# Mixing stages of a two-block network: order of ScalarE's root and table load, VectorE's rests and scans, and the size of the sum's pieces

## The reference, cut to what matters

```python
def hybrid_mixer(h, ...):
    proj = h @ w_in                       # 1024 -> 512 + 1280 + 1280 + 1024 + 1024
    u_pool, u_lru, u_gelu, g_logits = ...
    y_pool = pool_mixer(u_pool, ...) @ w_pool_up
    v = causal_depthwise_conv(u_lru, conv_w, conv_b)
    y_lru = (rg_lru(v, ...) * gelu(u_gelu)) @ w_lru_up
    g = sigmoid(g_logits)                 # g_pool, g_lru
    return (g_pool * y_pool + g_lru * y_lru) @ w_out

def rg_lru(u, w_a, b_a, w_x, b_x, lam):   # per head of 128, 10 heads
    r = sigmoid(u @ w_a + b_a);  i = sigmoid(u @ w_x + b_x)
    log_a = -8 * r * softplus(-lam)
    a = exp(log_a);  mult = sqrt(-expm1(2 * log_a))
    h_t = a_t * h_{t-1} + mult_t * i_t * u_t   # a scan over the tokens
    return h
```

## Time and profile before

| | us |
|---|---|
| median of 3 runs (lowest to highest) | 3142.77 (3141.48 to 3145.83) |
| profiled execution | 3143.91 |
| its span | 3142.2 |
| TensorE busy | 3015.3 (96%) |
| VectorE busy | 1566.0 (50%) |
| ScalarE busy | 1071.4 (34%) |
| GpSimd busy | 224.5 (7%) |

### The profile page before, as it was taken

The page is one execution under the profiler, slowest core; times in us unless marked ns, Lnnn a source line. Parts: engine busy times, 40 slices in busy tenths (PEclk is TensorE's granted clock), DMA queues, the critical chain, the costliest instruction groups (busy, mean ns, idle before and its releaser), DMA issues.

```text
span 3142.2 us, 42567 instructions
## 1 busy us (share of the span) xinstructions
PE 3015.3 (96%) x17368; PEld 2082.8 (66%) x17368; DVE 1566.0 (50%) x2551; ACT 1071.4 (34%) x1514; POOL 224.5 (7%) x262
## 2 busy tenths in 40 slices
PE   6999999999998989999999998999999999999998
PEld 5985444444443964444444445998879989897898
DVE  6764334444443673322234224557765555578554
ACT  3432222222223552222222224335543343464433
POOL 0300111111110001111111110000000000000000
PEclk9989999999999989999999999999999999999999
DMA  9836689999995537787879875554345555445453
GB/s 340 240 141 266 258 332 370 360 384 367 368 361 210 178 121 281 296 314 308 327 307 355 322 295 188 188 187 160 136 162 186 187 182 187 165 143 187 154 188 107
DMA packets 274332, 770.43 MB, mean 245 GB/s; under 512 B 36929, under 2 KB 186577, under 8 KB 210929
## 3 DMA queue, kind: packets, MB, share of 16 engines
q1 hardware_dynamic: 236016, 715.17, 61.6%
q0 software_dynamic: 29232, 45.43, 4.2%
q10 hardware_dynamic: 8912, 7.40, 0.8%
HBM read 924.08 MB, written 1.05 MB: 294 GB/s over the span
## 4 chain that ended last, share of the span: by engine, by line
PE 88%; DVE 7%; ACT 3%; issue 1%; DMA 1%; DVEq 0%; ACTq 0%
PE G L1421 21%; PE U L1441 6%; PE B L1441 5%; PE G L1207 5%; PE G L1208 5%; PE G L1209 5%; PE U L1207 4%; PE U L1208 4%; PE U L1209 4%; PE Y L1207 4%; PE Y L1208 4%; PE Y L1209 4%; PE Y L1452 2%; PE Y L1451 2%; PE M L1401 2%; PE U L1401 1%
## 5 line engine op out<-in xcount | busy, mean ns | idle before, releaser
L1796 DVE TENSOR_TENSOR part_lo<-ring,part_hi 128x2048 fp32r<-128x2048 f32 x240 | 547.8, 2288 | 389.8 <-ACT part_hi L868 388.1
L1421 PE MATMUL G<-wide,gathered 128*64 128x512 f32 x2368 | 680.9, 595 | 0.0
L868 ACT ACTIVATE part_hi<-ring 128x2048 fp32r<-128x2048 f32 x240 | 459.4, 1915 | 492.0 <-PE Y L1209 288.4
L1421 PEld LDWEIGHTS G<-wide,gathered 128*64 128x64 f32 x2368 | 207.4, 137 | 257.7 <-issue 257.7
L1421 PE MATMUL G<-arena,gathered 128*64 128x512 f32 x704 | 312.4, 596 | 0.0
L1207 PE MATMUL G<-h_hi,part_hi 128*128 128x256 f32 x1024 | 296.6, 290 | 10.9 <-DVE h_lo L1844 10.9
L1208 PE MATMUL G<-h_lo,part_hi 128*128 128x256 f32 x1024 | 295.1, 288 | 0.0
L1209 PE MATMUL G<-h_hi,part_lo 128*128 128x256 f32 x1024 | 294.7, 288 | 0.0
L1207 PE MATMUL U<-h_hi,part_hi 128*128 128x256 f32 x1024 | 289.8, 283 | 0.4 <-ACT arena L1158 0.3
L1208 PE MATMUL U<-h_lo,part_hi 128*128 128x256 f32 x1024 | 289.5, 283 | 0.0
L1209 PE MATMUL U<-h_hi,part_lo 128*128 128x256 f32 x1024 | 289.4, 283 | 0.0
(11 more groups left out here) (482 smaller groups left out, 5361.9 us busy)
## 6 DMA issues: line engine op xcount, KB each, us to landing
ring<-in_ffn_w_up_dram SPq DMA_DIRECT2D x88, 1024.0 KB, 5.3
arena<-in_moe_w_down_dram SPq DMA_DIRECT2D x86, 1024.0 KB, 7.3
wide<-in_moe_w_gate_dram SPq DMA_DIRECT2D x84, 1024.0 KB, 7.0
wide<-in_moe_w_up_dram SPq DMA_DIRECT2D x84, 1024.0 KB, 9.3
arena<-in_moe_w_gate_dram SPq DMA_DIRECT2D x44, 1024.0 KB
arena<-in_moe_w_up_dram SPq DMA_DIRECT2D x44, 1024.0 KB
ring<-in_ffn_w_down_dram SPq DMA_DIRECT2D x44, 1024.0 KB, 4.8
wide<-in_moe_w_down_dram SPq DMA_DIRECT2D x42, 1024.0 KB, 8.0
```

The source lines that it names most:

```text
L868: eng.activation(part_hi[:, n % SPLIT, :], ring[:, slot, :], ACT.Copy).then_inc(hi_ready, 1)
L1421: last = mm(bank["G"][rows], lhsT=gathered[p // 2 % 2][:, k, at:at + SLOTS], rhs=units[tile][:, :, k, :], start=(k == 0), stop=(k == K - 1 ...
L1796: eng.tensor_tensor(part_lo[:, n % SPLIT, :], ring[:, slot, :], part_hi[:, n % SPLIT, :].bitcast(F32), ALU.subtract).then_inc(lo_ready, 1)
```

## The change

On ScalarE: the rounding of unit 11 moves from behind unit 8 to behind the gates; a sigmoid of one column is put ahead of the gates; the root moves from behind the rounding of unit 20 (`q == 1`) to behind that of unit 19 (`q == 0`). On TensorE: the four banks G, U, B, M are waited for one by one, each ahead of its own piece, in units 12 and 20; unit 26 signals each of its pieces; the first unit behind the sum waits for the two halves of its rows apart. On VectorE: the low part of unit 11 moves behind the product with the gates, that of unit 21 ahead of the product with the gelu; the sum is made in four pieces of 512 columns; the first split is made in two halves of 256 columns.

```diff
-        b.book("half", f"lru_{l}")
+        b.book("half", f"lru_{l}", 3)
@@ ScalarE
-                def projected(f):
+                def projected(f, more=True):
...
-                    next_hi()
+                    if more:
+                        next_hi()
                 for f in range(IN_FIRST):
-                    projected(f)
+                    projected(f, f < IN_FIRST - 1)
+                eng.activation(stat[:, 61:62], eps[:, 0:1], ACT.Sigmoid)
                 for hd in range(LH):
...
+                next_hi()
                 projected(IN_FIRST)
...
                     wait_done(eng, unit + IN_UNITS + 4 + q)
                     next_hi()
-                    if q == 1:
+                    if q == 0:
                         eng.wait_ge(square_ready, l + 1)
                         eng.activation(tl, tl, ACT.Sqrt).then_inc(root_ready, 1)
@@ TensorE
-            def down_matmuls(parts, rows, first, end, to=None, halves=False):
+            def down_matmuls(parts, rows, first, end, to=None, halves=False, frees=None):
...
+                        if first and frees:
+                            wait_free(eng, "GUBM"[2 * t + half], frees)
...
-                for bk in "GUBM":
-                    wait_free(eng, bk, f"gp_{l}")
                 for q in range(4):
-                    down_matmuls(wait_unit(unit + 12 + q), h_rows(q), q == 0, q == 3, spread)
+                    down_matmuls(wait_unit(unit + 12 + q), h_rows(q), q == 0, q == 3, spread, frees=f"gp_{l}")
...
-                for bk in "GUBM":
-                    wait_free(eng, bk, f"yp_{l}")
...
-                                 halves=q == LRU_UNITS - 1)
+                                 halves="each" if q == LRU_UNITS - 1 else False)
...
+                def first_split(c):
+                    if c == 0:
+                        eng.wait_ge(first_rows, l + 1)
+                    else:
+                        eng.wait_ge(rows_ready, down + 7 + 1)
+                    return rows_hi[:, (down + 7) % 2, c, :], rows_lo[:, (down + 7) % 2, c, :]
+
                 for q in range(4):
-                    down_matmuls(wait_unit(unit + 27 + q), split_rows(down + 7 + q), q == 0, q == 3,
+                    down_matmuls(wait_unit(unit + 27 + q), split_rows(down + 7 + q) if q else first_split, q == 0, q == 3,
@@ VectorE
+            def split_first(src, n, read):
+                wait_done(eng, read)
+                hi, lo = rows_hi[:, n % 2], rows_lo[:, n % 2]
+                link(eng.tensor_copy(hi[:, 0, :], src[:, 0, :]))
+                eng.tensor_tensor(lo[:, 0, :], src[:, 0, :], hi[:, 0, :].bitcast(F32), ALU.subtract).then_inc(first_rows, 1)
+                eng.tensor_copy(hi[:, 1, :], src[:, 1, :]).then_inc(rows_round, 1)
+                eng.wait_ge(rows_round, n + 1)
+                eng.tensor_tensor(lo[:, 1, :], src[:, 1, :], hi[:, 1, :].bitcast(F32), ALU.subtract).then_inc(rows_ready, 1)
...
-                next_lo()
                 for hd in range(LH):
                     wait_drained(eng, gate_bank(hd), f"gates_{l}", hd // 2)
                 link(eng.tensor_tensor(ia, ia, vconv, ALU.mult))
-                next_lo(2)
+                next_lo(3)
...
+                next_lo()
                 link(eng.tensor_tensor(gl, gl, vconv, ALU.mult))
-                next_lo(2)
+                next_lo()
...
-                eng.wait_ge(half_done, b.at["half", f"lru_{l}"] + 1)
-                for t in range(TT):
-                    if t:
+                for j, (t, half) in enumerate(HALVES):
+                    if j < 3:
+                        eng.wait_ge(half_done, b.at["half", f"lru_{l}"] + j + 1)
+                    else:
                         wait_done(eng, unit + 26)
-                    for j in (2 * t, 2 * t + 1):
-                        s = mark(eng.tensor_tensor(quarter(glru, j), quarter(glru, j), quarter(Y, j), ALU.mult))
-                    eng.wait_ge(dve_step, s)
-                    eng.tensor_tensor(gpool[:, t, :], gpool[:, t, :], glru[:, t, :], ALU.add).then_inc(sum_ready, 1)
+                    hs = slice(half * HALF, (half + 1) * HALF)
+                    link(eng.tensor_tensor(quarter(glru, j), quarter(glru, j), quarter(Y, j), ALU.mult))
+                    o = eng.tensor_tensor(gpool[:, t, hs], gpool[:, t, hs], glru[:, t, hs], ALU.add)
+                    if half:
+                        o.then_inc(sum_ready, 1)
+                    else:
+                        mark(o)
                 for q, bk in enumerate("GUBM"):
                     wait_full(eng, bk, f"turned_{l}")
-                    split(bank[bk][:], down + 7 + q, unit + 25 + q)
+                    if q == 0:
+                        split_first(bank[bk], down + 7, unit + 25)
+                    else:
+                        split(bank[bk][:], down + 7 + q, unit + 25 + q)
```

More of the change, by code:

```diff
@@ L466, in build @@
         sum_ready = sem("sum_ready")
+        first_rows = sem("first_rows")
         half_done = sem("half_done")
@@ L1260, in down_matmuls @@
                             last.then_inc(half_done, 1)
-                    if halves is True and t == 0:
-                        last.then_inc(half_done, 1)
                 last.then_inc(unit_done, 1)
@@ L1726, in _ @@
                 down = b.at["down", f"mix_{l}"]
-                for bk in "GUBM":
-                    wait_free(eng, bk, f"yp_{l}")
                 for q in range(POOL_UNITS):
-                    down_matmuls(wait_unit(unit + 20 + q), split_rows(down + q), q == 0, q == POOL_UNITS - 1, spread)
+                    down_matmuls(wait_unit(unit + 20 + q), split_rows(down + q), q == 0, q == POOL_UNITS - 1, spread,
+                                 frees=f"yp_{l}")
                 wait_drained(eng, "Y", f"gl_{l}")
```

## The result

The changed kernel takes 3119.69 us in the median (3118.24 to 3121.79, four runs) against 3142.12 us (3140.84 to 3145.83, four runs) of the kernel before: 22.4 us less, a ratio of 0.9926 with a 95% interval of 0.9912 to 0.9939. The forecast was 3121. The profiled execution took 3120.01 us with a span of 3118.5, 23.7 less than the span before.

A forecast was written before the change was run, and what follows sets the result against it. TensorE bounds the kernel (88% of the span), so only its pauses count: 1.12 + 0.89 + 5.76 + 1.15 + 0.55 + 1.6 = 11.07 us a stage, 22.1 for both, from 3143.9, less 1.1: 3121 us, range 3117 to 3127.

The forecast's parts named there:

- Part 1: Gates on ScalarE: sigmoid table loaded ahead, unit 11's rounding behind the gates, so they begin earlier; gain 1.12 us a stage.
- Part 2: Unit 12 on TensorE: banks waited for one by one, so the 0.7 us pause goes; gain 0.89 us a stage.
- Part 3: Units 20 and 21: earlier root and scans remove TensorE's waits and the low clock; gain 5.76 us a stage.
- The margin of 2.3 us for unit 20: Unit 20's low part on VectorE done at 2258.1, TensorE asking at 2260.4: met by 2.3 us.
- my list of signs: Signs expected in the profile after, among them root about 7 us sooner against unit 19's end, sum waits 0.3 and 0.4.
- Rival B: VectorE is late with unit 20: 3127 us if late by 2 us, 3130 if by 3; chance 0.08.
- Parts 4 and 5: Behind unit 26: sum in shorter pieces gains 1.15 us a stage, first split in halves ahead of unit 27 gains 0.55.
- Part 6: Units 27 and 28: with the pause cut to 3.0 us the clock stays full; gain 1.6 us a stage, bounds 0 and 1.7.
- Rival A: The clock still falls behind the sum, ahead of unit 27: 2 x 1.6 us less gain, 3124 us; chance 0.15.
- C: Change doesn't do what it says: load stays ahead of first real sigmoid, or first gates wait otherwise; 3123 us; chance 0.04.
- D: Slower: ScalarE's wait for the square ahead of unit 20's rounding holds up the weights too; 3145 us; chance 0.01.
- the 2 us allowed: Allowance of 2 us either way for clock falls and rises at other moments at the later norms; an estimate.

The follow-up runs named there:

- experiment 5: Changed kernel without the one-column sigmoid ahead of the gates, unit 11's rounding still behind them: 3117.62 us.
- experiment 6: Changed kernel with unit 11's rounding back ahead of the gates, the one-column sigmoid kept behind it: 3125.51 us.
- experiment 7: Changed kernel with all four banks waited for ahead of unit 12 again: 3121.23 us.
- experiment 2: Changed kernel with the root back behind the rounding of unit 20: 3131.31 us in its one run.
- experiment 11: Kernel before with the eight turns of the sum's first half done twelve times over, a long pause full of turns: 3157.74 us.
- experiment 12: Kernel before with ten extra copies holding up VectorE ahead of the second half's products, a long pause nearly empty of turns: 3154.95 us.
- experiment 1: Kernel before with one edit, the root behind the rounding of unit 19 instead of unit 20: 3128.35 us against 3142.95, ratio 0.9961.
- experiment 10: Changed kernel with the sum and the first split back in large pieces: 3124.62 us.
- experiment 9: Changed kernel without the early sigmoid, both splits ahead of low parts, gates over four banks instead of two: 3115.61 us against 3142.91, ratio 0.9912.
- experiment 4: Changed kernel with VectorE splitting unit 29's rows ahead of unit 30's low part instead of behind it: 3119.35 us.

## Why the prediction was right

| step | forecast | measured in the first stage |
|---|---|---|
| 1, rounding behind the gates | 1.12 | 1.12 (11.66 to 10.54) |
| 2, banks one by one | 0.89 | 0.89 (18.23 to 17.34) |
| 3, root and scans | 5.76 | 6.07 (3.47 + 2.60) |
| 4 and 5, sum and split | 1.70 | 1.66 (4.72 to 3.06) |
| 6, clock behind the sum | 1.6 | 1.51 (24.22 to 22.71) |
| sum | 11.07 | 11.25 |

- Part 1 was right in size and named the right cause in passing (the rounding leaves the place to the load). Its heading, the sigmoid ahead, was the wrong one: experiment 5 takes it away and loses nothing, experiment 6 takes the move away and loses 1.21. The cover for unit 11 was 5.6 us, as forecast: its low part ends at 2204.74, and TensorE asks at 2210.32.
- Part 2: 0.89, or 0.97 when it is undone alone, because unit 12 to 20 then also loses 0.07 (43.62 for 43.55).
- Part 3 is the main term from both sides: alone it brings 5.43 us a stage, taken away it costs 4.8 to 5.0. The margin of 2.3 us for unit 20 was 2.3. It came out 0.31 over the forecast. Of this 0.07 belongs to part 2 (experiment 7), and the rest is slips in my sum: the 16.70 us began at the wait and so left out the overlap of 0.16, and two units take 10.88 us, not 10.94. By the measured pieces the clock's share is then about 1.8 us, not 1.6 (2.60 less the 0.6 + 0.16 of pause); experiment 2, which has no wait before unit 21, shows 1.60 and 1.78. The root is ready 5.4 us sooner against unit 19's end (10.46 us ahead of TensorE's asking for unit 20 instead of 5.03), not about 7 us as in my list of signs; that figure leaves out that unit 19's end comes 2.01 us sooner too. Rival B did not come about: in units 14 to 17 the low parts are done 1.1 us or more ahead, as forecast, and the four-bank version shows no wait there either.
- Parts 4 and 5: the sum ends 1.45 us behind unit 26; the split's two operations are 0.42 each, as taken. The waits are 0.63 and 0.40, where I had said 0.3 and 0.4: the first eight turns are through 0.87 us behind unit 26, sooner than I took, so more of the time until the sum is there shows as a wait. The two pieces are as forecast: the second eight turns begin 1.50 us behind unit 26 instead of 2.63 (1.13, forecast 1.15), and the wait for the split is 0.53 shorter (forecast 0.55).
- Part 6 was right in number, and in part by luck. That turns count was shown (11, 12). That the shorter pause is what brings the clock back was not: the pause of 4.7 us was followed by the low clock in two stages of two in the kernel before and in none of four in experiments 1 and 10. The early root alone had already brought the 1.5 us back (experiment 1), and undoing the short pause did not lose it (experiment 10); with a late root the short pause brought it too (experiment 2). So the 1.51 us in the table is a gain of the whole change, and no single edit owns it. Behind the pause of 3.06 us the clock fell in none of 16 stages (the changed kernel and experiments 2 to 7 and 9, two stages each). How often it falls behind the long one in runs without a profile stays open, so the 3 us of two stages may be more than the mean gain.
- Rival A did not come about, in none of the 16 stages; C was true in its letter (the early sigmoid does nothing) and not in its price; D has nothing for it, the square is ready 0.7 us before ScalarE asks. The chances of the cases add up to 1.00 without the 0.04 for a failure that I don't see, a slip that changes no conclusion.
- Outside of the stages: from unit 0 to the gates the changed kernel's profile takes 0.17 and 0.15 us longer (55.02 to 55.19 in the first stage), with the granted clock in the first 5 us at 0.65 for 0.68; whether that is the change's doing wasn't tried. The span is 1.5 us shorter still than the two stages explain (2 x 11.1 of 23.7): 0.9 ahead of the first mixing stage, where the programs are alike, -0.9 between the two and 1.5 behind the second. That is within the 2 us allowed; its cause wasn't tried either.

## What to carry to other kernels

When one engine bounds the kernel, list its waits in the stage, follow each to the instruction that ended it, and ask what stood ahead of that instruction in its own engine's order; here moving one root past one rounding gave half of the gain. A wait that is removed may only uncover the next link of the same chain one unit later (experiment 4), so follow the chain to its end before the edit. Measure small edits by marks inside the stage, and do not book a microsecond of clock as an edit's gain from one profile: here either of two edits removed the same fall, and only taking each away alone showed it.

## What the runs showed of the hardware that I had not expected

- A table load runs when ScalarE reaches it and does not wait for the operand of its function: in experiment 5 it is done 0.69 us before the bank is full. Loading a table "ahead" needs a free place in the order, not an instruction.
- Float32 turns alone hold TensorE at 2.4 GHz for 12.9 us (experiment 11), where a pause with 16 of them falls to 1.2 GHz (experiment 12).
- The same pause of 4.72 us is followed by 1.2 GHz in one kernel and by 2.4 in another, and repeats so in both of a profile's stages. The totals of experiment 1 lie in two groups 5 to 7 us apart; its slower runs weren't profiled. Experiment 9, with the short pause, has two such groups 4 to 5 us apart, so this pause need not be the cause.
- The ring of TensorE and ScalarE over two banks costs 10.54 us for ten heads; over four its waits vanish, and ten heads take 8.44 us, all of it matmuls (experiment 9).
